# A modulation vector formed by row sums beside a feed-forward layer, and attention sinks as score columns

## The chip, the cores and the metric

The kernel runs on one core of one Trainium2 chip, in one launch. The metric is the device time in microseconds (us) of that launch. The kernel before was timed in three runs: 2712.57, 2717.24 and 2718.96 us, median 2717.24. One more execution was profiled. The engines are PE (TensorE; PEld is its weight load), DVE (VectorE), ACT (ScalarE), POOL (GpSimd) and SP (SyncE), which issues the weight loads. Sixteen DMA engines move data.

## The reference

Sequence 512, width 1024, all in float32. A first block has two layers. Layer 0 is feed-forward, an RWKV-7 time mix, feed-forward; layer 1 is feed-forward, sliding-window attention with sinks, feed-forward. A second block follows, whose normalization is modulated by a vector `mod` that depends on the input `c` alone. The two places that matter here:

```python
# in the attention: 16 heads, windows of 256 keys per 128 queries, one sink logit per head
sink = jnp.broadcast_to(sinks..., s.shape[:-1] + (1,))
p = jax.nn.softmax(jnp.concatenate([s, sink], axis=-1), axis=-1)[..., :-1]
o = jnp.einsum('bnkgqs,bnskd->bnqkgd', p, vb)

# at the start of the second block: c is (1, 1024), w_ada (1024, 3072)
mod = c @ w_ada[l] + b_ada[l]
shift, scale, gate = jnp.split(mod, 3, axis=-1)
h = rmsnorm(x, norm_gain[l]) * (1.0 + scale[:, None, :]) + shift[:, None, :]
...
x = x + gate[:, None, :] * (merged @ w_out[l])
```

## The kernel before, in words

Activations lie transposed: width over 128 partitions in 8 tiles of 512 positions. Weights come in units of 128x512 float32, 256 KB each. For each unit SP loads `w_raw` (a ring of 4), POOL splits it into a high part `w_hi` and the remainder `w_lo` (also rings of 4; lines L221, L222, L212), and PE multiplies: 4 output tiles by 3 products (high by high, high by low, low by high; L230, L231, L232), twelve matmuls per unit. `w_lo_ready` tells PE that a unit is split, `w_used` tells POOL that a place in the ring is free. DVE and ACT read the banks, apply norms and activations and split the results in the same way.

All engines run the layers in program order, each from its own written-out queue: feed-forward layers f0 to f3, the mix between f0 and f1, the attention `swa` between f2 and f3, the second block after f3. A feed-forward layer has 11 blocks of 8 units into `mid`, then 44 units of output projection in two halves. Its last three units are done bank by bank (`closing_products`, L250 to L252), so that a bank is complete early. The norm after a layer sums squares over partitions with matmuls against ones (L362), takes root and inverse, and spreads the inverse over partitions (L399). While this small chain runs, PE does a few matmuls whose results nobody reads (`unread`, L442). The next layer starts with `early_products` (L267, L268, L271), which take each tile as soon as DVE has updated it, and `norm_beside`, which puts the square sums of the next norm between products.

The attention runs 16 steps in a software pipeline. In iteration i, PE makes the scores of step i (L2017), transposes the probabilities of step i-3 (L2030) and multiplies the values of step i-4 (L2048). DVE adds the window mask and takes the row maximum (L2174, four per step), negates it (`neg`, L2179), adds the sink's exponential to the row sum (`den`, L2184), inverts it (`inv`, L2186) and copies half of the transposed probabilities (L2192). ACT takes the exponentials (L2119) and, for the sinks, two small ones of 128x2 per step (L2123), and copies the other half (L2112). POOL multiplies the probabilities by `inv` (L2216). All of POOL's divisions stand in its queue between two weight units.

The modulation vector is formed in the attention. `w_ada` is loaded by ACT's queue in 8 tiles of 128x3072 (rows of w_ada over partitions), two buffers. DVE multiplies each tile by a column of `c` and adds it to `ada_sum`, in four parts of 768 columns (L2154 for the first tile, L2151 for the others): 4 parts of tile 0 before the first step, 4 of tile 1 in iterations 0 and 1, one part in every second iteration from 4 to 18 (tiles 2 and 3), and the 16 parts of tiles 4 to 7 after the last step, beside the output projection of the attention. The sum over partitions is left to PE: 24 matmuls of `ada_sum` against one column of ones (L1996), each recorded as two. Ten stand among the norm chain at the end of the attention, each with an unread matmul (L1995), and 14 beside the first 7 units of f3. DVE then adds the bias (`mod`, L2222), and PE waits for that before `norm_beside` of f3 (`mod_ready`), because the bank is used again.

Of the kernel before, what the change touches and what calls it, by code (L numbers as in the profile page):

```python
# [64 lines left out]
def vector_table():  # L65
# [17 lines left out]
    c.add("c", KT)  # L83
# [37 lines left out]
def program(nc, xT, weights, vectors, masks_in, gather_in, spread_in, rows_in, window_in, ada_in, pos_in, rope_in, fold_in,  # L121
            tri_in, mask_a_in, mask_b_in, out):
    n_units = weights.shape[0]
    with ExitStack() as ctx:
# [457 lines left out]
        class Ffn:  # L582
            def __init__(self, number, layer, which, first_unit, x_tiles, updates, kv=None, after=None):
# [13 lines left out]
                self.after, self.inner = after, after is not None  # L597
                self.halved = {1: 1, 3: 3}.get(number, 0)

        def ffn_tensor(pe, s):  # L600
            odd = 1 - s.even

            def block(b, set_, n, i=None, k0=0):
                for k in range(k0, KT):
                    if b == 0 and s.kv is None:
                        early_products(pe, [o[:] for o in bank[set_]], k, s.x0, n + k, s.halved)
                        sum_square(pe, s.pre, k, bank[s.pre_at][0])
                        if s.after is not None and k < 7:
                            done = ada_products(pe, 10 + 2 * k, 12 + 2 * k)
                            if k == 6:  # L610
                                done.then_inc(ada_ready, 1)
# [85 lines left out]
        def ffn_scalar(act, s):  # L697
# [1255 lines left out]
        score = [mid_buffer(f"score{n}", [P, 2, 2, 2 * P]) for n in range(4)]  # L1953
        prob_t = [mid_buffer(f"prob_t{n}", [P, 2, T]) for n in range(2)]
        top, neg, total, sink_e, den, inv = (mid_buffer(n, [P, 4, 4]) for n in ("top", "neg", "total", "sink_e", "den", "inv"))
        ada_sum = mid_buffer("ada_sum", [P, 3 * D])
        ada_w = [mid_buffer(f"ada_w{n}", [P, 3 * D]) for n in range(2)]

        class Swa:
            def __init__(self, first_unit, x_tiles, updates):  # L1960
# [7 lines left out]
                self.after, self.inner, self.halved = None, False, 2  # L1968
# [3 lines left out]
        ada_ready = sem("ada_ready")  # L1972
        mod_ready = sem("mod_ready")
        qv = Steps("query_dve", [("q", k) for k in each])
        qa = Steps("query_act", [("bias", k) for k in each])
        av = Steps("ada_dve", [("ada", k, part_) for k in each for part_ in range(4)])
# [8 lines left out]
                               [(n, a) for a in step_at(i, 1) for n in ("den", "inv")] + [("turn", a) for a in step_at(i, 3)]])  # L1985
# [5 lines left out]

        def ada_products(pe, first, last, unread=None):
# [6 lines left out]
        def swa_tensor(pe, s):  # L1999
# [77 lines left out]
            for k in s.post.summed:  # L2077
                sum_square(pe, s.post, k, bank[s.post_at][0])
# [981 lines left out]
```

## Time and profile before

| | |
|---|---|
| runs, us | 2712.57, 2717.24, 2718.96 |
| the profiled execution, us | 2714.14 |
| its span, first to last instruction, us | 2712.0 |
| mean granted clock of TensorE | 0.985 |
| busy share of ACT, DVE, POOL | 23%, 40%, 72% |
| chain that ended last: PE, issue, DVE, POOL, ACT | 84%, 6%, 5%, 3%, 2% |
| loads of w_ada | 8 of 1536 KB, 7.0 us from issue to landing (median) |
| loads of weights | 778 of 256 KB, 2.6 us |

The span is what the rows below are read against; times in them are counted from its start. The busy share is an average over stages. A row of a timeline is start, length and operation; `[x <-Y]` behind it says that the engine sat idle for x us before it until Y had finished. Lengths of neighbouring instructions on one engine overlap a little, so distances between starts tell what one costs. In time, the attention with its query products lies at about 1676 to 1842 us and f3 behind it to about 2250 us. The granted clock is 1.00 where PE runs at the higher of its two levels.

### The profile page before, as it was taken

Reading aid. Unit: us, or ns where it says so; the run is one execution under the profiler, and the core shown is the slowest. Engines: PE = TensorE matmul, PEld = TensorE weight load, DVE = VectorE, ACT = ScalarE, POOL = GpSimd, SP = SyncE. Lnnn points to the kernel's source line nnn. Section 1 sums busy time; section 2 is a strip of 40 time slices with the busy share of each in tenths; the row PEclk is TensorE's granted clock in tenths of the full one; section 3 lists DMA queues with packets and bytes.
Section 4 is the critical chain, followed back from the end, with each engine's and each line's share of the span. In section 5 each row is a group of like instructions: output and inputs, shape, how many; then the busy total and the mean of one; then the engine's idle time right before and its main releaser. Section 6 shows DMA issues by size and latency. Waiting matters only on the chain.

```text
span 2712.0 us, 48113 instructions
## 1 busy us (share of the span) xinstructions
PE 2603.9 (96%) x17580; PEld 2116.9 (78%) x17580; DVE 1071.3 (40%) x1674; ACT 635.5 (23%) x1220; POOL 1956.0 (72%) x2573
## 2 busy tenths in 40 slices
PE   8999999988989999999999999889999999999998
PEld 6888887767877788888888888668888878777767
DVE  4222047884555622211522203876322233123354
ACT  2111025423443311101211102533111011354211
POOL 7888788873324688877788877676888858755675
PEclk9999999989999999999999999999999989999998
DMA  4333322210001233333333333342333323322212
GB/s 144 100 97 93 97 82 78 80 54 4 4 4 40 71 105 97 93 97 88 87 97 93 97 97 88 142 145 71 100 94 96 96 72 100 91 61 66 84 51 78
DMA packets 116790, 225.90 MB, mean 83 GB/s; under 512 B 13088, under 2 KB 13856, under 8 KB 115616
## 3 DMA queue, kind: packets, MB, share of 16 engines
q1 hardware_dynamic: 114624, 209.46, 26.6%
q10 hardware_dynamic: 2016, 14.22, 1.4%
q8 instruction: 121, 1.98, 0.3%
q14 instruction: 29, 0.24, 0.0%
HBM read 221.53 MB, written 2.10 MB: 82 GB/s over the span
## 4 chain that ended last, share of the span: by engine, by line
PE 84%; issue 6%; DVE 5%; POOL 3%; ACT 2%; DMA 0%; POOLq 0%; SPq 0%; DVEq 0%; ACTq 0%
PE bank L230 21%; PE bank L232 21%; PE bank L231 20%; PE bank L1480 1%; PE bank L362 1%; POOL w_hi L222 1%; PE bank L267 1%; PE bank L268 1%; PE bank L271 1%; POOL w_lo L212 1%; PE bank L1495 1%; PE bank L2462 1%; POOL w_hi L221 1%; PE bank L1430 1%; PE bank L1498 1%
## 5 line engine op out<-in xcount | busy, mean ns | idle before, releaser
L212 POOL TENSOR_TENSOR w_lo<-w_raw,w_hi 128x512 fp32r<-128x512 f32 x778 | 1051.5, 1352 | 63.6
L230 PE MATMUL bank<-x_hi,w_hi 128*128 128x512 f32 x1848 | 729.1, 395 | 6.3 <-POOL w_lo L212 4.3
L232 PE MATMUL bank<-x_hi,w_lo 128*128 128x512 f32 x1848 | 725.1, 392 | 0.0
L231 PE MATMUL bank<-x_lo,w_hi 128*128 128x512 f32 x1848 | 723.5, 391 | 0.0
L221 POOL TENSOR_TENSOR w_hi<-w_raw,ones 128x32 fp32r<-128x32 f32 x778 | 275.0, 354 | 452.6 <-PE bank L232 348.2
L222 POOL TENSOR_SCALAR w_hi<-w_raw 128x480 fp32r<-128x480 f32 x778 | 509.3, 655 | 0.0
L230 PEld LDWEIGHTS bank<-x_hi,w_hi 128*128 128x128 f32 x1848 | 347.5, 188 | 88.3 <-POOL w_lo L212 8.4
L232 PEld LDWEIGHTS bank<-x_hi,w_lo 128*128 128x128 f32 x1848 | 347.4, 188 | 76.1
L231 PEld LDWEIGHTS bank<-x_lo,w_hi 128*128 128x128 f32 x1848 | 347.5, 188 | 75.2 <-issue 0.2
L729 DVE TENSOR_TENSOR f<-bank,rstd 128x512 f32<-128x512 f32 x88 | 56.7, 686 | 624.0 <-PE bank L232 614.1
L232 PE MATMUL bank<-mid_hi,w_lo 128*128 128x512 f32 x656 | 257.2, 392 | 0.0
L231 PE MATMUL bank<-mid_lo,w_hi 128*128 128x512 f32 x656 | 256.8, 392 | 0.0
L230 PE MATMUL bank<-mid_hi,w_hi 128*128 128x512 f32 x656 | 256.2, 390 | 0.0
L705 ACT ACTIVATE f<-f 128x512 f32<-128x512 f32 x88 | 53.9, 632 | 717.5 <-DVE f L729 717.4
L231 PEld LDWEIGHTS bank<-mid_lo,w_hi 128*128 128x128 f32 x656 | 123.2, 188 | 27.4
L230 PEld LDWEIGHTS bank<-mid_hi,w_hi 128*128 128x128 f32 x656 | 123.2, 188 | 27.1
L232 PEld LDWEIGHTS bank<-mid_hi,w_lo 128*128 128x128 f32 x656 | 123.2, 188 | 26.3
L338 ACT ACTIVATE sq<-bank 128x512 f32<-128x512 f32 x35 | 20.4, 598 | 457.6 <-PE bank L232 224.0
L358 DVE TENSOR_TENSOR acc<-acc,sq 128x512 f32<-128x512 f32 x45 | 39.8, 885 | 209.1 <-ACT sq L338 208.8
L742 DVE TENSOR_TENSOR mid_lo<-f,mid_hi 128x512 f32 (+1 forms) x88 | 101.7, 1182 | 11.0 <-ACT mid_hi L710 10.9
L510 DVE TENSOR_SCALAR f<-bank,vec 128x512 f32<-128x512 f32 x20 | 14.9, 743 | 223.8 <-ACT sq L338 223.8
L1718 POOL TENSOR_TENSOR e_mat<-mab,masks 128x512 f32<-128x512 f32 x40 | 50.7, 1273 | 64.5 <-PE bank L1480 39.0
(479 smaller groups left out, 3669.9 us busy)
## 6 DMA issues: line engine op xcount, KB each, us to landing
w_raw<-weights SPq DMA_DIRECT2D x778, 256.0 KB, 2.6
ada_w<-ada_in ACTq DMA_DIRECT2D x8, 1536.0 KB, 7.0
h<-xT SPq DMA_DIRECT2D x4, 512.0 KB, 6.7
out<-f SPq DMA_DIRECT2D x8, 256.0 KB, 2.2
mask_b<-mask_b_in ACTq DMA_DIRECT2D x1, 640.0 KB, 3.9
spread<-spread_in SPq DMA_DIRECT2D x1, 512.0 KB, 7.8
window<-window_in ACTq DMA_DIRECT2D x1, 512.0 KB, 5.0
masks<-masks_in SPq DMA_DIRECT2D x1, 320.0 KB, 7.7
```

The source lines that it names most:

```text
L212: pool.tensor_tensor(w_lo[:, (n - 1) % RW, :], w_raw[:, (n - 1) % RS, :], w_hi[:, (n - 1) % RW, :].bitcast(F32), ALU.subtract).then_inc(w_ ...
L221: pool.tensor_tensor(w_hi[:, n % RW, 0:HEAD], w_raw[:, n % RS, 0:HEAD], ones[:, 0:HEAD], ALU.mult)
L222: pool.tensor_scalar(w_hi[:, n % RW, HEAD:], w_raw[:, n % RS, HEAD:], 1.0, 0.0, ALU.mult, ALU.add).then_inc(w_hi_ready, 1)
L230: pe.matmul(outs[m], w_hi[:, s, c], hi, start=first, stop=False)
L231: pe.matmul(outs[m], w_hi[:, s, c], lo, start=False, stop=False)
L232: done = pe.matmul(outs[m], w_lo[:, s, c], hi, start=False, stop=last)
L267: pe.matmul(o[:, t], w_hi[:, s, c], x_hi[:, k, t], start=k == 0 and t.start == 0, stop=False)
L358: dve.tensor_tensor(acc[:], acc[:], square_at(nm, j), ALU.add).then_inc(sq_used, 1)
L705: act.activation(g_buf[:, p, :], g_buf[:, p, :], ACT.Silu).then_inc(silu_ready, 1)
L729: dve.tensor_tensor(g_buf[:, p, :], bank[set_][p][:], rstd[:], ALU.mult).then_inc(bank_read, 1)
L742: dve.tensor_tensor(lo, u_buf[:, p, :], hi.bitcast(F32), ALU.subtract).then_inc(mid_lo_ready, 1)
L1718: pool.tensor_tensor(e_mat[:, u], mab[:, u], masks[:, l:l + 1, :].to_broadcast([P, 8, CH]), ALU.mult).then_inc(*cg.tell("e", m, l, u))
```

## The change

**The modulation.** `w_ada` is now laid out transposed: 24 tiles of 128x1024, where each partition holds one output of `mod` and its row of 1024 weights. `c` comes as a tile `cond`, repeated on all partitions. One `tensor_tensor_reduce` of 128x1024 on DVE multiplies a tile by `cond` and sums along the row, which gives one column of `mod`. This is done in f3: ACT loads `cond` and two tiles before its first block; behind each of the ten looped blocks DVE has two products and ACT two loads, each behind a wait for the product that frees the buffer; the last four products, the bias and the gain of the second block's norm stand behind the loop on DVE. In the loop the sums go through the small tile `root2` to `mod`. The matmuls against ones, their bank and the two waits for it go; the end of the attention now uses the same `output_tensor` as the other layers.

**The sinks.** Each row of the score tile gets one more column. DVE copies the sinks of the step's heads there before the mask (128x4, L2146 of the kernel after); the exponential of ACT runs over 257 columns instead of 256 and its row sum then includes the sink. The two exponentials of 128x2 and the addition `den` go.

```diff
         def norm_beside(pe, s, outs, n, last):
-            if s.after is not None:
-                pe.wait_ge(s.after, 1)
...
         def ffn_tensor(pe, s):
                         early_products(pe, [o[:] for o in bank[set_]], k, s.x0, n + k, s.halved)
                         sum_square(pe, s.pre, k, bank[s.pre_at][0])
-                        if s.after is not None and k < 7:
-                            done = ada_products(pe, 10 + 2 * k, 12 + 2 * k)
...
         def ffn_scalar(act, s):
+            if s.inner:
+                act.dma_start(cond[:], cond_in).then_inc(cond_loaded, 16)
+                for n in two:
+                    ada_load(act, n)
             block(0)
             with act.Fori(0, (FB - 1) // 2) as i:
                 for j in range(2):
                     block(1 + j, i)
+                    for n in two if s.inner else ():
+                        act.wait_ge(ada_done, count(2 * j + n + 1, i, 4))
+                        ada_load(act, 2 * j + n + 2, i)
+            if s.inner:
+                for n in range(LOOPED + 2, ADA):
+                    act.wait_ge(ada_done, n - 1)
+                    ada_load(act, n)
...
         def ffn_vector(dve, s):
             block(0, s.even)
+            if s.inner:
+                dve.wait_ge(cond_loaded, 16)
+                dve.memset(root2[:], 0.0).then_inc(ada_kept, 1)
             with dve.Fori(0, (FB - 1) // 2) as i:
-                block(1, 1 - s.even, i)
-                block(2, s.even, i)
+                for j, set_ in enumerate((1 - s.even, s.even)):
+                    block(1 + j, set_, i)
+                    for n in two if s.inner else ():
+                        ada_product(dve, 2 * j + n, i)
+            if s.inner:
+                for n in range(LOOPED, ADA):
+                    ada_product(dve, n)
+                ada_vector(dve)
...
-        score = [mid_buffer(f"score{n}", [P, 2, 2, 2 * P]) for n in range(4)]
+        score = [mid_buffer(f"score{n}", [P, 2, 2, 2 * P + 16]) for n in range(4)]
...
         def swa_tensor(pe, s):
-            pe.wait_ge(f_ready, s.h0 // 2 + 4)
-            pe.wait_ge(*av("ada", KT - 1, 3))
-            norm_sums(pe, s.post, bank[s.post_at][0])
-            for k in s.post.summed:
-                sum_square(pe, s.post, k, bank[s.post_at][0])
-            ada_products(pe, 0, 2, bank[SETA][3])
-            norm_wide(pe, s.post, bank[s.post_at][1])
-            ada_products(pe, 2, 10, bank[SETA][0])
+            output_tensor(pe, s)
...
         def swa_scalar(act, s):
                     for j in two:
                         for t in two:
-                            act.activation(score[a % 4][:, j, t, :], score[a % 4][:, j, t, :], ACT.Exp, ...)
-                    for j in two:
-                        c = KV + 2 * (a // 2) + j
-                        done = act.activation(sink_e[:, a % 4, 2 * j:2 * j + 2], neg[:, a % 4, 2 * j:2 * j + 2], ACT.Exp, bias=rows[:, c:c + 1])
+                            with_sink = score[a % 4][:, j, t, 0:2 * P + 1]
+                            done = act.activation(with_sink, with_sink, ACT.Exp, ...)
...
         def swa_vector(dve, s):
-            for part_ in range(4):
-                ada(0, part_)
...
+                    sinks = rows[:, KV + 2 * r:KV + 2 * r + 2].rearrange("p (j t s) -> p j t s", t=1, s=1).to_broadcast([P, 2, 2, 1])
+                    dve.tensor_copy(score[a % 4][:, :, :, 2 * P:2 * P + 1], sinks)
...
-                    dve.tensor_tensor(den[:, a % 4, :], total[:, a % 4, :], sink_e[:, a % 4, :], ALU.add).then_inc(*ad.tell("den", a))
-                    dve.wait_ge(*ad("den", a))
-                    dve.reciprocal(inv[:, a % 4, :], den[:, a % 4, :]).then_inc(*ad.tell("inv", a))
+                    dve.reciprocal(inv[:, a % 4, :], total[:, a % 4, :]).then_inc(*ad.tell("inv", a))
...
-                if i < 2:
-                    ada(1, 2 * i)
-                    ada(1, 2 * i + 1)
-                elif i % 2 == 0 and 4 <= i <= 18:
-                    ada(2 + (i - 4) // 8, (i - 4) // 2 % 4)
             low(KT - 1)
-            for k in range(4, KT):
-                for part_ in range(4):
-                    ada(k, part_)
             output_vector(dve, s)
...
+        def ada_product(dve, n, i=None):
+            dve.wait_ge(ada_loaded[n % 2], count(16 * (n // 2 + 1), i, 32))
+            total_ = mod[:, n:n + 1] if i is None else root2[:, n:n + 1]
+            if i is not None and n == 0:
+                dve.wait_ge(ada_kept, count(1, i, 1))
+            dve.tensor_tensor_reduce(out=ada_w[n % 2][:], in0=ada_w[n % 2][:], in1=cond[:], scale=1.0, scalar=0.0, op0=ALU.mult, op1=ALU.add,
+                                     accum_out=total_).then_inc(ada_done, 1)
+            if i is not None and n == 3:
+                dve.wait_ge(ada_done, count(4, i, 4))
+                dve.tensor_tensor(mod[:, bass.ds(i * 4, 4)], root2[:], ones[:, 0:4], ALU.mult).then_inc(ada_kept, 1)
```

DVE in the attention, from the end of one step to the first mask operation of the next, before (`score_136` and so on are the four score buffers, `ISA` is the masking operation or the read of its maximum):

```order
L2179 TENSOR_SCALAR neg<-top 128x4
L2184 TENSOR_TENSOR den<-total,sink_e 128x4
L2186 RECIPROCAL inv<-den 128x4
L2192 COPY prob_t_141<-bank 128x512
L2151 SCALAR_TENSOR_TENSOR ada_sum<-ada_w_149,vec,ada_sum 128x768
L2174 ISA score_137,top<-bank,window,rows 128x256
```

and the same place in the changed kernel:

```order
L2154 TENSOR_SCALAR neg<-top 128x4
L2159 RECIPROCAL inv<-total 128x4
L2165 COPY prob_t_141<-bank 128x512
L2146 COPY score_139<-rows 128x4
L2149 ISA score_139,top<-bank,window,rows 128x256
```

The addition and the accumulation are gone, and a copy of the sinks stands in front of each step's first mask operation, behind the inverse that lets POOL start.

PE at the end of the attention, from the square sums to the first products of f3, before:

```order
L362 MATMUL bank<-ones,acc 128x64 x4
L362 MATMUL bank<-ones,sq_last 128x64 x4
L1995 MATMUL bank<-ones,ident 128x128
L1996 MATMUL bank<-ones,ada_sum 128x1
L1995 MATMUL bank<-ones,ident 128x128
L1996 MATMUL bank<-ones,ada_sum 128x1
L399 MATMUL bank<-ident,rinv 128x128 x4
L1995 MATMUL bank<-ones,ident 128x128
L1996 MATMUL bank<-ones,ada_sum 128x1
```

and in the changed kernel:

```order
L438 MATMUL bank<-ones,ident 128x128
L361 MATMUL bank<-ones,acc 128x64 x4
L361 MATMUL bank<-ones,sq_last 128x64 x4
L438 MATMUL bank<-ones,ident 128x128 x2
L398 MATMUL bank<-ident,rinv 128x128 x4
L438 MATMUL bank<-ones,ident 128x128 x6
L266 MATMUL bank<-x_hi,w_hi 128x256
```

Before, eight pairs of an unread matmul and a modulation product follow the spread inverse (the last row shown begins them); now six unread matmuls do, and f3's products come next.

## Rows read from the trace of the kernel before

**Rows 1.** The page's first part: busy us (share of the span), instructions.

```profile
PE 2603.9 (96%) x17580; PEld 2116.9 (78%) x17580; DVE 1071.3 (40%) x1674; ACT 635.5 (23%) x1220; POOL 1956.0 (72%) x2573
```

**Rows 2.** Two windows: us, busy us (instructions) by engine, clock, DMA share, GB/s.

```profile
1750.00:1780.00 30.00, 24.38 (x210) 16.88 (x208) 28.18 (x109) 27.23 (x103) 18.58 (x36) 1.00 0.15 54
1900.00:2000.00 100.00, 100.00 (x438) 82.05 (x438) 25.71 (x34) 10.45 (x17) 84.09 (x113) 1.00 0.34 98
```

**Rows 3.** The waits of PE, 1680 to 1900 us: line, releaser, total, times, longest.

```profile
PE bank L2030 <- DVE q_t L2144: 5.4, 1, 5.4
...
PE bank L250 <- POOL w_lo L212: 3.8, 2, 2.0
...
PE bank L230 <- DVE mod L2222: 1.8, 1, 1.8
```

**Rows 4.** Timeline of DVE, two steps of the attention: start, us, operation, [idle before].

```profile
1754.07 1.03 DVE L2151 SCALAR_TENSOR_TENSOR ada_sum<-ada_w,vec,ada_sum 128x768 f32<-128x768 f32 x1
...
1756.75 0.17 DVE L2179 TENSOR_SCALAR neg<-top 128x4 f32<-128x4 f32 x1
1756.83 0.16 DVE L2184 TENSOR_TENSOR den<-total,sink_e 128x4 f32<-128x4 f32 x1
1757.03 0.18 DVE L2186 RECIPROCAL inv<-den 128x4 f32<-128x4 f32 x1
...
1760.88 1.02 DVE L2151 SCALAR_TENSOR_TENSOR ada_sum<-ada_w,vec,ada_sum 128x768 f32<-128x768 f32 x1
```

**Rows 5.** Timeline of PE and DVE, the head of the attention.

```profile
1727.35 2.00 PE L2017 MATMUL bank<-k_sh,q_t 64*128 64x256 f32 x16
...
1729.93 0.47 DVE L2174 CUSTOM_DVE_ANT_0 score<-bank,window,rows 128x256 f32<-128x256 f32 x1
...
1734.78 1.54 PE L2030 MATMUL bank<-ident,score 128*128 128x128 f32 x6 [5.43 <-DVE q_t L2144]
```

**Rows 6.** Timeline of POOL and DVE where both read SBUF in the attention.

```profile
1730.44 1.62 POOL L2216 TENSOR_SCALAR score<-score,inv 128x128 f32<-128x128 f32 x4
...
1731.65 0.43 DVE L2179 TENSOR_SCALAR neg<-top 128x4 f32<-128x4 f32 x1
...
1753.66 2.61 POOL L2216 TENSOR_SCALAR score<-score,inv 128x256 f32<-128x256 f32 x4 [1.54 <-DVE inv L2186]
```

**Rows 7.** The tile ada_sum, DVE's row: ns min/median/max; then POOL's timeline.

```profile
L2151 DVE SCALAR_TENSOR_TENSOR ada_sum<-ada_w,vec,ada_sum x28: 1006/1056/2066, 1722.6 to 1817.0; 128x768 f32<-128x768 f32 x28
...
1796.74 0.25 POOL L221 TENSOR_TENSOR w_hi<-w_raw,ones 128x32 fp32r<-128x32 f32 x1 [1.85 <-PE bank L232]
...
1818.24 0.97 POOL L221 TENSOR_TENSOR w_hi<-w_raw,ones 128x32 fp32r<-128x32 f32 x1
```

**Rows 8.** Timeline of PE, the output projection of the attention.

```profile
1793.57 0.50 PE L230 MATMUL bank<-x_hi,w_hi 128*128 128x512 f32 x1
...
1823.92 0.51 PE L250 MATMUL bank<-x_hi,w_hi 128*128 128x512 f32 x1 [1.77 <-POOL w_lo L212]
...
1826.91 0.79 PE L250 MATMUL bank<-x_hi,w_hi 128*128 128x512 f32 x1 [2.02 <-POOL w_lo L212]
```

**Rows 9.** Timeline of PE, square sums that end one layer and open the next.

```profile
1671.64 1.00 PE L362 MATMUL bank<-ones,acc 128*128 128x64 f32 x8
...
1704.44 1.10 PE L362 MATMUL bank<-ones,acc 128*128 128x64 f32 x8 [1.36 <-DVE acc L358]
...
1835.45 1.00 PE L362 MATMUL bank<-ones,acc 128*128 128x64 f32 x8
...
1873.68 1.00 PE L362 MATMUL bank<-ones,acc 128*128 128x64 f32 x8
```

**Rows 10.** The tile ada_sum, PE's row; then POOL in the last feed-forward layer.

```profile
L1996 PE MATMUL bank<-ones,ada_sum x48: 166/250/250, 1837.6 to 1864.5; 128*128 128x1 f32 x48
...
1904.61 0.25 POOL L221 TENSOR_TENSOR w_hi<-w_raw,ones 128x32 fp32r<-128x32 f32 x1
...
1906.77 0.25 POOL L221 TENSOR_TENSOR w_hi<-w_raw,ones 128x32 fp32r<-128x32 f32 x1
```

More of the change, by code:

```diff
@@ L82, in vector_table @@
     c.add("final", KT)
-    c.add("c", KT)
     return c
@@ L582, in program, with __init__ @@
         class Ffn:
-            def __init__(self, number, layer, which, first_unit, x_tiles, updates, kv=None, after=None):
+            def __init__(self, number, layer, which, first_unit, x_tiles, updates, kv=None, inner=False):
                 self.kv, self.rs = kv, new_rstd()
@@ L596, in __init__ @@
                 self.pre, self.post = Norm(KT, () if kv is None else ODD, kept=True), Norm(KT, (7,), late=True)
-                self.after, self.inner = after, after is not None
+                self.inner = inner
                 self.halved = {1: 1, 3: 3}.get(number, 0)
@@ L1967, in __init__ @@
                 self.gain_in, self.gain_out, self.bias, self.half, self.kv = "norm12", "norm13", "b_o", 1.0, None
[L1968 removed]
+                self.inner, self.halved = False, 2
         window_loaded = sem("window_loaded")
         ada_loaded = [sem(f"ada_loaded{n}") for n in range(2)]
[L1972 to L1973 removed]
+        cond_loaded = sem("cond_loaded")
+        ada_done = sem("ada_done")
+        ada_kept = sem("ada_kept")
         qv = Steps("query_dve", [("q", k) for k in each])
         qa = Steps("query_act", [("bias", k) for k in each])
[L1976 removed]
         STEPS = 2 * KT
@@ L1990, in swa_blocks @@
             return [(t, kt) for t, kt in (((0, 0), (1, 0), (1, 1)) if x == 0 else ((0, 0), (0, 1), (1, 0), (1, 1)))]
-        def ada_products(pe, first, last, unread=None):
-            for m in range(first, last):
-                if unread is not None:
-                    pe.matmul(unread[:, 0:P], ident[:], ones[:], start=True, stop=True)
-                done = pe.matmul(bank[SETA][2][:, m:m + 1], ada_sum[:, m * P:(m + 1) * P], ones[:, 0:1], start=True, stop=True)
-            return done
         def swa_tensor(pe, s):
@@ L2295, in program @@
         pa = Steps("proj_act", ["sin"] + [(n, m) for n, tiles in PROJ + BESIDE + GATES for m in range(tiles)])
-        pv = Steps("proj_dve", ["gain"] + [("norm", k) for k in each] +
+        pv = Steps("proj_dve", ["mod", "gain"] + [("norm", k) for k in each] +
                    ["float", "angle", "near", "steps", "less1", "less2", "less3", "phase", "clip", "one"])
@@ L2369, in second_vector @@
         def second_vector(dve, s):
-            dve.scalar_tensor_tensor(out=gain_s[:], in0=mod[:, KT:2 * KT], scalar=1.0, in1=vec[:, VEC.at["gain2"]:VEC.at["gain2"] + KT],
-                                     op0=ALU.add, op1=ALU.mult).then_inc(*pv.tell("gain"))
             dve.wait_ge(*ip("wide"))
@@ L2835, in program @@
         swa = Swa(f2.end, 8 * KT, 4)
-        f3 = Ffn(3, 1, 1, swa.end, 10 * KT, 5, after=mod_ready)
+        f3 = Ffn(3, 1, 1, swa.end, 10 * KT, 5, inner=True)
         second = Second(f3.end, 11 * KT, 6)
```

58 lines of the change are left out of this document (23 added, 35 removed).

## The prediction

> **What bounds the kernel now.** I read the page's busy shares first, then windows by stage, then the waits of PE, then timelines of the stages that the change touches. PE is busy for 96% of the span [rows 1], so nearly all work elsewhere is free, and only two kinds of time can be won: PE's own instructions and the few stretches in which PE stands still or in which an engine sets its pace. In the last feed-forward layer PE has no gap: 438 matmuls in 100 us, so a unit of twelve takes 2.74 us [rows 2]. In the attention it is different. From 1750 to 1780 us PE is busy for 24.38 of 30 us, DVE for 28.18 and ACT for 27.23 [rows 2]: DVE sets the pace there. The waits of PE around the attention show three that involve the modulation: 5.4 us at the attention's head for a query that DVE writes late, 3.8 us for POOL's low weights in the output projection, 1.8 us for the tile mod at the start of the last feed-forward layer [rows 3].
>
> **Part 1: the attention's loop (saves 3.5 us).** In the loop DVE works without a gap, and the distance between two modulation steps, which is two attention steps, is 1760.88 - 1754.07 = 6.81 us [rows 4]. The change takes out of such a pair one accumulation (1.0 us) and two additions that form the denominator (from 1756.83 to 1757.03, 0.20 us each [rows 4]), and adds two copies of the sinks, 128x4, which I price like the negation of the same size, 1756.75 to 1756.83, 0.08 us from start to start [rows 4]. DVE's own work falls to 6.81 - 1.00 - 0.40 + 0.16 = 5.57 us. The copies have a hidden price. POOL's division of a step takes 1.62 or 2.61 us in four instructions [rows 6], 4.23 us per pair, so POOL is working in about two thirds of the loop, and the copy stands just where it works: behind inv, which starts it. The negation that fell into such a division, at 1731.65, took 0.43 us, against 0.17 us outside one [rows 4, 6]. So a small operation waits for the POOL instruction under way, 0.41 or 0.65 us long. I take 0.3 us per copy, 0.6 us per pair; nothing and 0.65 us per copy are the ends. That gives 6.2 us of DVE per pair. The other engines leave room: PE's share gives 24.38 / 30 x 6.81 = 5.5 us, and ACT's gives 6.2 us, from which the two pairs of sink exponentials go. Because the chain crosses from DVE to ACT and back, I take 0.5 us saved per pair, not 0.6. Eight accumulations stand in the loop with seven distances between them, so 3.5 us. Ends: 0 (ACT or the chain keeps the old pace) to 7 x 1.0 = 7 us (copies never blocked).
>
> The Trainium skill (SBUF — State Buffer, Who interferes with whom) says that a copy or a scalar operation in a two-port mode takes the port pair that VectorE shares with GpSimd for the whole instruction, and whoever is second is blocked until the first is done. The trace agrees for the negation, 0.43 against 0.17 us. A copy from SBUF to SBUF is of that kind, so by this rule the copies are the part of the change that speaks against it; without the rule the part would be worth the 7 us of its upper end.
>
> **Part 2: the head of the attention (saves 1.5 us).** Four accumulations leave DVE in the first two steps. PE waits 5.43 us until 1734.78 for the last queries, which DVE scales after the third step's scores [rows 5]. The third mask began at 1729.93, while its scores, the first half of sixteen matmuls from 1727.35 that took 2.00 us, were there at about 1728.4 [rows 5]. Everything behind it on DVE can move up by that 1.5 us only; the rest of the wait stays. Ends: 0.5 and 2.5 us (two denominators go too, and POOL no longer loses time to the first accumulations).
>
> **Part 3: the output projection (saves 6.0 us).** From 1793.57 to the square sums at 1835.45 lie 41.88 us [rows 8, 9]; 13 weight units are in it, which at 2.74 us are 35.6 us. The loss is 6.3 us. It has one cause, and the change removes it: sixteen accumulations and more run back to back on DVE from there, and under them POOL needed 1818.24 - 1796.74 = 21.5 us for six units, 3.58 us each [rows 7], where a unit without them takes 1906.77 - 1904.61 = 2.16 us [rows 10]. At 3.58 us POOL is slower than PE's 2.74, uses up its lead, and PE waits 1.77 and 2.02 us [rows 8]. Behind the second wait a matmul's record is 0.79 us instead of 0.51: the rest of the loss is matmuls at the lower clock. Without the accumulations POOL is the faster one, and next in line is nothing but PE itself. 6.0 us; ends 3.8 (waits alone) and 6.3.
>
> **Part 4: the passage into the last feed-forward layer (saves 5.0 us).** Before, 24 products of 128x1 (48 recorded matmuls, 0.25 us each [rows 10]) stand on PE: ten between fillers and fourteen beside the first units, and then PE waits 1.8 us for mod [rows 3]. The passage from the feed-forward layer into the attention has the same code without them. From square sums to square sums it takes 1704.44 - 1671.64 = 32.80 us; the one at hand takes 1873.68 - 1835.45 = 38.23 us [rows 9]. The difference, 5.4 us, is what can go. What is late next is DVE's sum of squares, as the 1.36 us wait at 1704.44 shows [rows 9]; since DVE works at its own speed there I hold back 0.4 us. Ends: 1.8 (the wait for mod alone) and 5.4.
>
> **Part 5: the last feed-forward layer (costs nothing).** DVE gets 24 multiply-and-sum operations of 128x1024, two per block of eight units. None is in the trace; by length the accumulation of 768 columns gives 1.06 x 4/3 = 1.4 us, at its slowest 2.07 x 4/3 = 2.8 us [rows 7]. DVE is busy for a quarter of this layer [rows 2], and PE needs a bank read only one block, 21.9 us, later, so DVE's time is hidden. POOL's is the question. In the projection it lost 6 x (3.58 - 2.16) = 8.5 us under 21.5 us of accumulations, 0.40 us per us. Two operations of 1.4 us then cost POOL 1.1 us per block, at worst 2.2 us; it is busy for 84.09 of 100 us [rows 2], which leaves 3.5 us per block. Hidden. If the cover went, every us beyond 3.5 would cost 11 blocks x 1 us. The loads are 1 MB per block, 48 GB/s on top of 98 [rows 2]. They are issued by ACT, which now waits for DVE's product behind each block; behind that wait stand the next block's silu operations, whose inputs come from DVE behind the same product, so nobody waits longer. The last four products, the addition of the bias and the gain stand on DVE before output_vector, 44 units (120 us) before PE's square sums: hidden. Ends: a gain is excluded (work is only added); loss up to the case of the third rival.
>
> The same page and section say that an operation with two SBUF inputs, as the multiply-and-sum is, blocks a GpSimd instruction that reads SBUF, for its full length. By that rule POOL would lose up to 2.8 us per block instead of 1.1, still under the spare 3.5, so the sum stays; the third rival is that rule with slower operations. The rows show 0.40 us lost per us, not 1, because both engines have gaps and DVE waits as well.
>
> **Sum.** 3.5 + 1.5 + 6.0 + 5.0 = 16.0 us, all on PE's path, because behind it PE has no slack until the end. The profiled execution took 2714.14 us (span 2712.0): 2698.1 us. The median of the runs, 2717.24 us, is 3.1 us above that execution, which would give 2701.2. I predict 2700 us.
>
> **Rivals.** First, the copies of the sinks are not blocked by POOL: DVE's pair is then 5.57 us and the chain through ACT and PE about 5.8, so the loop saves 7 x 1.0 = 7 us: 2696. For it: a negation in the loop is short, 0.17 us [rows 4]; against it: that one stands before inv, when POOL has finished, and the copy stands after. Second, DVE's relief doesn't reach PE, in the loop or in the passage: ACT, busy for 27.23 of 30 us, keeps the loop's pace, or the sum of squares keeps most of the passage. Then only 0 to 1 us of part 1 or 1.8 us of part 4 remain: 2703 with one of them, 2706 with both. ACT's high share speaks for it, the removed exponentials against. Third, on the other side: in the last feed-forward layer the new operations run at the slow end, 2.8 us each, and shut POOL out for their full length. 5.6 us per block against 3.5 us spare is 2.1 us x 11 = 23 us lost, PE waits for low weights throughout: 2700 + 23 = 2723, slower than before. It decides from 1.75 us of POOL's time per operation on. The slowest accumulation in rows 7 speaks for such lengths, the 0.40 measured under the densest stretch against.
>
> **Chances.** Forecast 0.55, first rival 0.17, second 0.22, third 0.06. A measurement of this kernel tells about 0.2%, 5.4 us, from no change, so faster means under 2711.8. The first two rivals are faster too. The forecast's ends sum to savings of 6 and 21 us, which are hardly reached together. Range 2692 to 2710. Faster 0.91, same 0.05, slower 0.04 (part of the third rival falls short of it).
>
> **What would show it.** The distance of two prob_t copies of one kind in the attention near 6.3 us, and copies of the sinks with records of 0.3 us or more; first transposes at about 1733.3; no wait for w_lo in the output projection, with square sums 35.9 us after the unit that began at 1793.57; 33 us from there to the next square sums; in the last feed-forward layer no wait of PE for w_lo beyond what was there, POOL busier by some 5 of 100 us. I would be wrong if PE waits for w_lo in that layer, if the loop's pace stays at 6.8 us, or if a new wait stands in the passage.

## The result, and the profile after

The changed kernel takes 2680.2 us (median of 4 runs, 2677.0 to 2687.6) against 2714.9 us before (4 runs, 2711.9 to 2719.0): ratio 0.987, 95% interval 0.985 to 0.989. Faster was right; the time of 2700 us was 20 us too high, and 2680 us lies outside the range of 2692 to 2710. The profiled execution took 2679.1 us, its span 2677.3 us, 34.7 us less than the one before.

First the page's busy shares after the change. PE is still busy for 96% of the span, but for 26.0 us less than before [rows 1], of which the removed products of the modulation (48 recorded matmuls of 0.25 us, [rows 10]) explain 12 us at most. That was the first sign that something else had changed.

```profile
PE 2577.9 (96%) x17530; PEld 2108.5 (79%) x17530; DVE 1071.9 (40%) x1696; ACT 629.2 (24%) x1188; POOL 1959.0 (73%) x2573
```

Next the two windows that answer to [rows 2]: 30 us inside the attention's loop and 100 us of the last feed-forward layer; the columns are us, busy us (instructions) of PE, PEld, DVE, ACT and POOL, clock, DMA share, GB/s.

```profile
1730.00:1760.00 30.00, 29.42 (x256) 20.64 (x254) 28.66 (x128) 26.66 (x94) 16.86 (x39) 1.00 0.01 2
1900.00:2000.00 100.00, 100.00 (x443) 82.81 (x442) 40.58 (x56) 11.21 (x18) 91.07 (x113) 1.00 0.50 146
```

The first line goes the way that was forecast, and further: the loop gets 256 matmuls through in the time of 210, where a pair of steps in 6.3 instead of 6.81 us would give 227. PE is busy for 29.42 of the 30 us there, against 24.38 before, so the loop now runs nearly as fast as PE's own work allows. The second line was not forecast: PE was without a gap before and is without a gap now, and yet it does 443 matmuls instead of 438, beside more work of DVE and POOL, not less. The first feed-forward layer, which stands 1300 us ahead of anything that the change moves, shows the same (next fence: 200 us of it, before and then after).

```profile
100.00:300.00 200.00, 200.00 (x876) 1.00 0.33 96
...
100.00:300.00 200.00, 200.00 (x884) 1.00 0.34 97
```

The waits of PE from 1660 to 1850 us answer to [rows 3]: those for w_lo in the projection and for mod are gone (0.3 us are left), the one for q_t fell from 5.4 to 3.7 us.

```profile
PE bank L2036 <- DVE q_t L2129: 3.7, 1, 3.7
PE bank L361 <- DVE acc L357: 2.8, 2, 1.4
...
PE bank L229 <- POOL w_lo L211: 0.3, 1, 0.3
```

Last, the timeline of PE at the stages' borders, the counterpart of [rows 5, 8, 9].

```profile
1659.96 1.00 PE L361 MATMUL bank<-ones,acc 128*128 128x64 f32 x8
...
1692.64 1.10 PE L361 MATMUL bank<-ones,acc 128*128 128x64 f32 x8 [1.44 <-DVE acc L357]
...
1722.32 0.90 PE L2036 MATMUL bank<-ident,score 128*128 128x128 f32 x3 [3.71 <-DVE q_t L2129]
...
1777.15 0.50 PE L229 MATMUL bank<-x_hi,w_hi 128*128 128x512 f32 x1
...
1812.88 1.00 PE L361 MATMUL bank<-ones,acc 128*128 128x64 f32 x8
...
1845.49 1.10 PE L361 MATMUL bank<-ones,acc 128*128 128x64 f32 x8 [1.37 <-DVE acc L357]
...
2181.91 1.00 PE L361 MATMUL bank<-ones,acc 128*128 128x64 f32 x8
```

When the attention begins, the changed kernel is already 11.7 us ahead (1659.96 against 1671.64). From border to border the 34.7 us come to: 14.4 us in the four feed-forward layers (3.2, 4.7, 3.4 and 3.1), 10.8 us in the attention (131.01 to 120.24), 5.6 us in the passage (38.23 to 32.61), 3.5 us behind the last feed-forward layer, 0.4 us elsewhere. The attention and the passage are where the forecast had its 16 us; the rest was not in it.

### The profile page after: what moved, and what is told of

The parts are those of the page before. It is cut to its first block, busy times and chain, and to the rows that moved or that the text cites. A ratio compares the mean times of both kernels' runs of the same rounds, so it can differ in the third digit from the quotient of the medians.

```text
span 2677.3 us, 48059 instructions
## 1 busy us (share of the span) xinstructions
PE 2577.9 (96%) x17530; PEld 2108.5 (79%) x17530; DVE 1071.9 (40%) x1696; ACT 629.2 (24%) x1188; POOL 1959.0 (73%) x2573
## 4 chain that ended last, share of the span: by engine, by line
PE 84%; issue 5%; DVE 5%; POOL 3%; ACT 2%; DMA 0%; POOLq 0%; SPq 0%; DVEq 0%; ACTq 0%
PE bank L229 21%; PE bank L230 21%; PE bank L231 21%; PE bank L1492 1%; PE bank L361 1%; POOL w_lo L211 1%; POOL w_hi L221 1%; PE bank L266 1%; PE bank L1507 1%; PE bank L267 1%; PE bank L270 1%; PE bank L2448 1%; PE bank L1442 1%; PE bank L1510 1%; PE bank L2439 1%
## 5 line engine op out<-in xcount | busy, mean ns | idle before, releaser
L337 ACT ACTIVATE sq<-bank 128x512 f32<-128x512 f32 x35 | 20.4, 598 | 441.5 <-PE bank L251 218.8
L745 DVE TENSOR_TENSOR mid_lo<-f,mid_hi 128x512 f32 (+1 forms) x88 | 101.2, 1176 | 11.1 <-ACT mid_hi L702 10.9
```

The lines of the kernel that those rows point to most:

```text
L745: dve.tensor_tensor(lo, u_buf[:, p, :], hi.bitcast(F32), ALU.subtract).then_inc(mid_lo_ready, 1)
```

## The experiments

**Theory A.** A line of the diff that the part shown above leaves out takes the entry `c` out of the vector table (`c.add("c", KT)`); 279 columns become 271, and the tile `vec` shrinks from 1152 to 1088 bytes. Every tile behind it in SBUF moves by 64 bytes: x_hi from byte 70080 to 70016, mid_hi from 119232 to 119168. The weights, ahead of it, stay at 41088 and 49280. A matmul of 512 columns then costs less because of where its moving operand starts. **Theory B:** the pace is the chip's or the instruction stream's, not the placement's. The first four runs separate them. Each group of runs was made beside runs of the kernel before, whose median was 2713.8 to 2720.4 us from group to group; so a few us between versions of different groups say little, and the count of matmuls in the same 200 us (from 100 to 300 us, inside the first feed-forward layer) tells more.

e1, the kernel before with eps behind the tables:

```diff
-        eps = sb("eps", [P, 1])
...
         out_bias = sb("out_bias", [P, KT])
+        eps = sb("eps", [P, 1])
```

> The kernel before with nothing changed but the place of one small table (eps) in SBUF, so that x_hi, x_lo and the middle values, the moving operands of the 512-column matmuls, start at a multiple of 128 bytes (byte 70016 instead of 70080) as they do in the changed kernel, while the weights keep their bytes. Theory A (18 us of the saving come from the moving operands' addresses, which the shorter vector table shifted): about 18 us less than before, 2697 us, with 443 instead of 438 matmuls of PE in 100 us of a feed-forward layer. Theory B (the faster matmul comes from the chip's state or from the instruction stream of the changed program): the time of before, 2715 us.

Measured: 2703.0 us (2699.5 to 2705.9) against 2713.8, ratio 0.996 (0.9945 to 0.9973), and 884 matmuls in the 200 us. The four feed-forward layers are 14.4 us shorter; its mix layer took 498.6 us against 492.9, which took part of it back in the profiled execution. Over all profiles of this study that layer lies between 489.7 and 502.8 us without a pattern in the placements. A holds; its 18 us was too much for this run.

e2, the changed kernel with the old addresses. This is the clean measure of what the change does by itself.

```diff
         vec = sb("vec", [P, VEC.n])
+        place[0] += 64
```

> The changed kernel with 64 bytes left empty behind the vector table, so that every tile behind it has the address of before. Theory A (addresses): about 18 us more than the changed kernel, 2698 us, which is what the change's own parts give (16 us less than before). Theory B (state or instruction stream): 2680 us as the changed kernel.

Measured: 2699.3 us (2694.1 to 2701.8), ratio 0.995 (0.9935 to 0.9968), 19 us above the changed kernel. The feed-forward layers are back at 876 matmuls, as before. B is out. The borders of its stages, for the forecast's own terms:

```profile
1704.69 0.77 PE L362 MATMUL bank<-ones,acc 128*128 128x64 f32 x5 [1.35 <-DVE acc L358]
...
1732.93 1.54 PE L2037 MATMUL bank<-ident,score 128*128 128x128 f32 x6 [3.72 <-DVE q_t L2130]
...
1774.39 0.50 PE L230 MATMUL bank<-x_hi,w_hi 128*128 128x512 f32 x1
...
1823.68 0.89 PE L362 MATMUL bank<-ones,acc 128*128 128x64 f32 x7
...
1856.41 1.10 PE L362 MATMUL bank<-ones,acc 128*128 128x64 f32 x8 [1.29 <-DVE acc L358]
...
2196.04 1.00 PE L362 MATMUL bank<-ones,acc 128*128 128x64 f32 x8
```

e3 moves the middle values alone, e4 the weights alone (the line stands before `w_hi`; eps goes behind the tables, so that x stays):

```diff
         f = sb("f", [P, KT, T])
+        place[0] += 64
```
```diff
+        place[0] += 64
         w_hi = sb("w_hi", [P, RW, UC], F32R)
```

> The changed kernel with x_hi and x_lo where they are, and only the middle values (mid_hi, mid_lo, the moving operand of every second-half unit of a feed-forward layer) moved by 64 bytes. Theory A, by the share of matmuls that read the middle values (about 1970 of some 8000, 2.6 ns each): 5 us more than the changed kernel, 2685 us, lost in the second half of each feed-forward layer alone. Theory B: 2680 us. A third theory, that it is another tile behind the vector table: 2680 us here, 2698 us in the run beside it.

> The changed kernel with x and the middle values where they are, and w_hi and w_lo, the stationary operands, moved by 64 bytes. If only the moving operand's start counts, 2680 us as the changed kernel. If the weight side counts as much as the moving one, its loads are hidden beside the matmuls before them, so at most some us: up to 2700 us when a weight load's reads collide in the same way.

Measured: e3 2682.6 us (2679.9 to 2684.9), 882 matmuls, its first feed-forward layer 337.5 us against 336.3 (after) and 339.5 (before): the loss stays with the matmuls that read the middle values. e4 2731.1 us (2730.6 to 2735.6), 859 matmuls, slower than the kernel before. So the weights' place counts, and more than x's, which no theory had.

**Theory R**, that only the distance between the two operands counts, against A (each for itself). e5 puts 64 bytes before w_hi and leaves all behind it shifted too; e6 puts the tile mod (128 bytes) there; e7 orders the small tables so that ident, ones, masks, spread and gather start at multiples of 128; e8 moves x and the middle values by 32.

```diff
+        place[0] += 64                     # e5, before w_hi
...
+        mod = sb("mod", [P, 3 * KT])       # e6, before w_hi
...
+        eps = sb("eps", [P, 1])            # e7, before ident
+        place[0] += 128                    # e7, before masks, instead of 64
+        gain_s = sb("gain_s", [P, KT])     # e7, before spread; it also moves gn_eps of the mix layer
...
+        place[0] += 32                     # e8, before sq; again before masks
```

> The changed kernel with 64 bytes left empty before w_hi, so that the weights and everything behind them, x and the middle values too, start 64 bytes off a multiple of 128. Moving x alone cost 19 us and moving the weights alone cost 51 us. Theory A (each operand pays for its own start): more than 2731 us, about 2750 us if the prices add up. Theory R (only the distance between the two operands counts): 2680 us, as the changed kernel, where both start at a multiple of 128.

> The changed kernel with 128 bytes more before w_hi, so that weights, x and middle values start at multiples of 256 (before: 128 past one). If a multiple of 128 is all that counts: 2680 us. If a still wider boundary counts: less, and more than 443 matmuls in 100 us of a feed-forward layer; one of 512 columns every 0.2257 us against 0.2133 us for 512 columns at 2.4 GHz leaves room for up to 100 us.

> The changed kernel with its small tables put in another order, so that nearly every tile of 512 bytes and more starts at a multiple of 128 (identity, ones, masks, spread, gather are added to x, the middle values and the weights). If starts matter for small matmuls, transposes and vector operations too: some us less than the changed kernel, 2672 to 2678 us, won between 405 and 898 us (the mix layer). If only the 512-column matmuls' operands matter: 2680 us.

> The changed kernel with x and the middle values 32 bytes past a multiple of 64, the weights as they are. If the price goes by whether the start is a multiple of 128: as with 64 bytes, 2699 us. If it goes by 64-byte pieces that a read touches: more than that, up to 2720 us.

Measured: e5 2677.5 us (2676.3 to 2683.8), ratio 0.9855 (0.9836 to 0.9875), and 884 matmuls, with both operands 64 past a multiple of 128. A falls in its first form: no start is good or bad by itself. R holds. e6 2684.1, e7 2683.6 us: neither a wider boundary nor aligned small tables are worth anything. e8 2734.2 us.

e9 and e10 split the change by its parts: e9 is the changed kernel with the sinks handled as before, e10 the kernel before with the sinks as score columns.

```diff
-                    dve.tensor_copy(score[a % 4][:, :, :, 2 * P:2 * P + 1], sinks)     # e9; e10 adds it
...
+                    dve.tensor_tensor(den[:, a % 4, :], total[:, a % 4, :], sink_e[:, a % 4, :], ALU.add).then_inc(*ad.tell("den", a))
```

> The changed kernel with the sinks handled as before (no copies of them into the scores, two exponentials of 128x2 per step on ACT, an addition before the reciprocal), the modulation and all addresses of x, middle values and weights as in the changed kernel. By the prediction's first part the sinks' new form costs DVE 0.2 us more per pair of steps than it takes away (0.6 against 0.4), so without it the loop is 1.4 us shorter: 2679 us. By the rival (the saved exponentials of ACT and the short copies are what made the pace 5.95 instead of 6.3 us per pair): 0.35 us per pair more, 2683 us.

> The kernel before with the sinks as score columns, the modulation left in the attention, and the vector table left at its length, so that all starts are those of before. By the prediction: 1.4 us more in the loop, 2716 us, and no change in a feed-forward layer (438 matmuls in 100 us). If the faster matmul came with the sinks' part of the change: 2697 us. If copies are cheap: 2 us less, 2713 us.

Measured: e9 ratio 0.988 (0.9864 to 0.9903), which can't be told from the changed kernel's 0.987; by borders its attention takes 120.75 us against 120.24, and the profiles of the six other versions with the changed kernel's instructions there and distance 0 lie between 120.26 and 120.35. e10 ratio 1.000 (0.9989 to 1.0013), 875 matmuls in 200 us. The sinks are worth 0.5 us once the modulation is gone. While the modulation is there they bring nothing that can be measured: e10's attention took 132.98 us against 131.01, but the passage behind it 36.84 against 38.23, and e1, with the sinks as before, had 132.46 us in the attention. Its copies of the sinks had a median of 0.30 us against 0.21 in the changed kernel. So within the noise all of the change's own gain is the modulation.

e11 and e12 reach two more distances from x's side (small tables moved from ahead of x to behind out_bias: eps and root, or eps alone).

```diff
-        eps = sb("eps", [P, 1])                # e11 and e12: from ahead of sq
-        root = sb("root", [P, TT])             # e11 alone
...
         out_bias = sb("out_bias", [P, KT])
+        eps = sb("eps", [P, 1])
+        root = sb("root", [P, TT])
```

> The changed kernel with x and the middle values 128 bytes lower, the weights as they are: the distance from w_hi to x_hi is 128 past a multiple of 256. Theory P128 (the distance counts modulo 128): 2680 us and 443 matmuls in 100 us. Theory P256 (it counts modulo 256; +64 cost 19 us, -64 cost 51 us, so they are not alike): another number than 443, between 430 and 442, 2685 to 2735 us.

> The changed kernel with x and the middle values 64 bytes lower and the weights as they are: the same distance (-64) as in the run that moved the weights up by 64, reached from the other side. If the distance decides, as the run with both shifted says: 2731 us and 430 matmuls in 100 us of a feed-forward layer. If the place of the weights themselves cost the 51 us there: 2699 us and 438, as with x moved up.

Measured (one run each): e11 2721.3 us, 862 matmuls in 200 us; e12 2732.9 us, 859, as in e4, which has the same distance from the other side. The period is not 128.

e13 moves x by 1280 bytes (vec, eps, root and rinv go behind out_bias), e14 by 32 and e15 by 160, all downwards. e16 puts one more product ahead of each product of the modulation.

```diff
-        vec = sb("vec", [P, VEC.n])            # e13; it also moves eps, root and rinv
-        eps = sb("eps", [P, 1])                # e14; e15 moves eps, root and rinv
+        place[0] += 32                         # e14 and e15, before sq
...
+            dve.tensor_tensor_reduce(out=spare[:, 0:896], in0=ada_w[n % 2][:, 0:896], in1=cond[:, 0:896], scale=1.0, scalar=0.0, op0=ALU.mult,
+                                     op1=ALU.add, accum_out=spare[:, 896:897]).then_inc(spare_done, 1)
```

> The changed kernel with x and the middle values 1280 bytes lower (some small tables stand behind them now), the weights as they are: the distance from w_hi to x_hi is a multiple of 512, not 256 past one as in the changed kernel. Period 256: 2680 us and 443 matmuls in 100 us. Period 512 with a still better place: fewer us than 2676, over 443 matmuls. Period 512 with 256 as the good place: 430 to 440 matmuls, 2695 to 2735 us.

> The changed kernel with x and the middle values 32 bytes lower: distance -32 from that of the changed kernel. So far +32 cost 54 us, +64 19 us, -64 51 us, -128 41 us. If only multiples of 64 and more are good places: 430 matmuls in 100 us, 2733 us. If the price grows with the distance below 0: 436 to 440, about 2705 us.

> The changed kernel with x and the middle values 160 bytes lower: distance -160, which is +96 with a period of 256. If places that are no multiple of 64 are all bad: 430 matmuls in 100 us and 2733 us. If the price is a smooth curve between +64 (438) and +128 (432): 435 matmuls, about 2712 us.

> The changed kernel with each of the 24 products of the last feed-forward layer preceded by another one of 896 columns, whose result nobody reads. By the prediction's last part GpSimd has 3.5 us to spare per block of 21.9 us and loses about 1.1 us to two products, so that four still hide: 2680 us, the layer 336.4 us, GpSimd near 97 of 100 us. By the third rival (each product shuts GpSimd out for its full length, 1.3 us here): 4 x 1.3 = 5.1 us per block, 1.6 us over the spare time, 11 blocks: 17 us more, 2697 us, with waits of PE for w_lo.

Measured: e13 2685.2 us (2683.9 to 2686.3), 884 matmuls: the period is 256. e14 2733.0, e15 2737.6 us (one run each). e16 2693.7 us (2691.0 to 2698.3), the last feed-forward layer 347.35 us against 336.42: the cover of part 5 does run out. 100 us of that layer and the waits of PE in it:

```profile
2000.00:2100.00 100.00, 95.69 (x412) 78.03 (x412) 66.48 (x85) 11.27 (x17) 97.17 (x101) 0.98 0.48 142
...
PE bank L229 <- POOL w_lo L211: 7.8, 8, 1.8
```

POOL is full at 97 of 100 us, PE waits for low weights 8 times, and some of what follows runs at a lower granted clock (0.98). The forecast had given 2680 us here, the third rival 2697.

e17 moves w_lo alone by 64 bytes (eps behind the tables, so that x stays), e18 the mix layer's own buffers.

```diff
+        place[0] += 64                                                              # e17
         w_lo = sb("w_lo", [P, RW, UC], F32R)
...
+        where["r_arr"] = where["mid_hi"] + 64                                       # e18
```

> The changed kernel with w_lo alone moved up by 64 bytes, w_hi, x and the middle values as they are. All three matmuls of a product were 0.0070 us slower when both weights were moved. Theory L (a load of weights collides with the stream of the matmul before it): only the load of w_lo, which happens under the stream of x_lo in the matmul x_lo, w_hi, is at the bad distance, and a third of the 51 us is lost: 2697 us, 438 or 439 matmuls in 100 us, with one of the three records longer. Theory O (the distance between the two operands of one matmul counts, with the weights read again during it): also a third, but the longer one is the matmul x_hi, w_lo. Theory S (any operand off its place slows all): 2731 us.

> The changed kernel with the mix layer's own buffers (r, k, v, u and what follows them) moved up by 64 bytes, which took them where the third run had them, and x, the middle values and the weights of all feed-forward layers at the good distance. The third run's mix layer took 489.7 us against 492.7 us. If that was placement: 3 us less than the changed kernel, 2677 us. If it was chance: 2680 us and more, the layer anywhere between 490 and 502 us as in the other runs.

Measured: e18 2683.8 us (2681.3 to 2686.1), its mix layer 497.3 us: e3's 489.7 was chance. e17 2722.2 us (one run), 867 matmuls. None of its three theories had that: one load in three is moved, and it loses 17 matmuls, where moving all weights lost 25. PE's groups in 200 us (line, operands, count, busy us, mean ns of one):

```profile
L232 PE MATMUL bank<-x_hi,w_lo 128*128 128x512 f32 x229 | 91.0, 397 | 0.0
L231 PE MATMUL bank<-x_lo,w_hi 128*128 128x512 f32 x228 | 89.4, 392 | 0.0
L230 PE MATMUL bank<-x_hi,w_hi 128*128 128x512 f32 x228 | 88.7, 389 | 0.0
```

The matmul that uses w_lo and the one under which w_lo is loaded are longer, the third has the 389 ns of the changed kernel. All loads keep 188 ns. The price sits where w_lo is involved; whether the load or the stream is held up is left open.

All placements together, x's start less w_hi's, modulo 256 (all four moving tiles and both weights have the same one, except in e17, and in e3, which is not in the table: x at 0, the middle values at 64, 882 matmuls, 337.5 us):

| distance | matmuls in 200 us | first feed-forward layer, us | runs |
|---|---|---|---|
| 0 | 884 | 336.3 | changed kernel, e1, e5, e6, e7, e9, e13, e16, e18 |
| 32 | 859 | 345.9 | e8 |
| 64 | 875 or 876 | 339.5 | kernel before, e2, e10 |
| 96 | 858 | 345.9 | e15 |
| 128 | 862 | 344.5 | e11 |
| 192 | 859 | 345.9 | e4, e12 |
| 224 | 859 | 345.9 | e14 |
| 0, w_lo 192 | 867 | 342.7 | e17 |

160 was not tried. The period rests on e11, which rules out 128, and on e13, which moves x by five times 256. No version measured beats the changed kernel: the ratios of e5, e7, e13 and e18 (0.9855 to 0.9876) have intervals that overlap its 0.987.

## Why the prediction was wrong

**The step that failed** is the sum: it took the five parts from the time before and left every other us as it was, "because behind it PE has no slack until the end". The diff's shorter vector table is an edit that the prediction gave no term. It has one: in the profiled spans 14.9 us (2692.2 of e2 less 2677.3), by the medians 19 us. Without it the changed kernel is e2, 2699.3 us, where the prediction said 2700; that they agree to a microsecond is in part luck, since the terms below were off by up to 0.6 us each and the kernel before ran at 2713.8 us beside e2, where the prediction started from 2717. The busy share of 96% was read as work that nothing could shorten. But a unit of twelve matmuls at 2.74 us was itself a slow one: 12 x 200 / 876 = 2.740 us, and 12 x 200 / 884 = 2.715 us at the good distance.

The forecast's own terms, best read on e2 (its borders above against [rows 5, 8, 9]):

- **Part 1, the loop**, forecast 3.5: 45.55 to 41.46 us, 4.1 saved. The loop ends where the first unit of the output projection starts; that line of the kernel before is:

```profile
1780.33 0.50 PE L230 MATMUL bank<-x_hi,w_hi 128*128 128x512 f32 x1
```

  The size is near, but by luck. Seven pairs were to save 0.5 us each. The copies of `prob_t`, one per step, show what happened (next fence: two copies of one kind in the kernel before, then two in e2). A pair fell from 6.81 us, in places 7.15, to 6.13 and 5.78 us, not to 6.3: over nine steps in the middle, 31.21 us (from 1746.68 to 1777.89) became 26.73 us (from 1745.20 to 1771.93), 1.0 us saved per pair. The first three steps gave 0.5 us back (9.94 us became 10.44), with PE at its lower clock from 1731.5 to 1738.3 us in e2, twice as long as before.

```profile
1753.48 0.68 DVE L2192 COPY prob_t<-bank 128x512 f32<-128x512 f32 x1
...
1760.29 0.68 DVE L2192 COPY prob_t<-bank 128x512 f32<-128x512 f32 x1
...
1757.09 0.69 DVE L2166 COPY prob_t<-bank 128x512 f32<-128x512 f32 x1
...
1763.22 0.69 DVE L2166 COPY prob_t<-bank 128x512 f32<-128x512 f32 x1
```

  So the pace came near the first rival's 5.8 us, and PE is nearly without a gap at it. The copies were priced at 0.3 us; over all 16 their median is 0.208 us, the longest 0.580. The timeline of DVE and POOL shows both lengths, each time while POOL is at its divisions:

```profile
1749.71 1.62 POOL L2181 TENSOR_SCALAR score<-score,inv 128x128 f32<-128x128 f32 x4 [1.10 <-DVE inv L2159]
1750.61 0.30 DVE L2146 COPY score<-rows 128x4 f32<-128x4 f32 x1
...
1752.89 1.85 POOL L2181 TENSOR_SCALAR score<-score,inv 128x256 f32<-128x256 f32 x4 [1.55 <-DVE inv L2159]
1753.33 0.16 DVE L2146 COPY score<-rows 128x4 f32<-128x4 f32 x1
```

  So a copy is longer at times, not always; the first rival had the better part of the truth. The second rival is wrong: DVE's relief reached PE.
- **Part 2, the head**, forecast 1.5: 30.34 to 28.24 us, 2.1 saved. In the changed kernel it is only 0.7: there PE's clock fell for a while behind its wait at 1692.64, shown by records of 0.63 us instead of 0.39 and starts 0.43 us apart instead of 0.23 (the lower of the two levels, 1.2 GHz; the granted clock reads 0.50 from 1694.0 to 1697.3 us). Eight matmuls at 0.2 us each are the 1.6 us that e2 doesn't lose. The change's instructions don't cause this, but its placement goes with it: all nine profiles with x and the middle values at distance 0 have the stretch, e1 with the instructions of before among them, and none of the eleven others. Why the clock falls there was not followed up. A term of that size hides under it.

```profile
1694.67 0.63 PE L229 MATMUL bank<-x_hi,w_hi 128*128 128x512 f32 x1
1695.10 0.63 PE L230 MATMUL bank<-x_lo,w_hi 128*128 128x512 f32 x1
...
1698.18 0.39 PE L231 MATMUL bank<-x_hi,w_lo 128*128 128x512 f32 x1
1698.41 0.39 PE L229 MATMUL bank<-x_hi,w_hi 128*128 128x512 f32 x1
```

- **Part 3, the output projection**, forecast 6.0: from the loop's end to the square sums 55.12 to 49.29 us, 5.8 saved, with 0.3 us of waits for w_lo left. Right, in place and size.
- **Part 4, the passage**, forecast 5.0: 38.23 to 32.73 us, 5.5 saved. DVE's sum of squares is late next by 1.3 us, as it was said; the 0.4 us held back were not needed.
- **Part 5, the last feed-forward layer**, forecast 0: 339.48 to 339.63 us. Right in the result, half right in the size. A product takes 1.26 to 2.35 us, median 1.57 (forecast 1.4 to 2.8). For POOL the next fence has the whole layer, before and after, with the same 365 instructions of POOL in it; so 24 products cost POOL 295.05 - 274.68 = 20.4 us, 0.85 us each, not 0.55. That is 1.7 us per block against 3.5 to spare. With four per block (e16) nothing is to spare, and the layer gets 10.9 us longer: the third rival was right that the cover can run out, and it lay one doubling away. Its price was too high: by e16's expectation its rule gave 17 us, and a further product cost POOL (317.19 - 295.05) / 24 = 0.92 us, not its full length.

```profile
1873.68:2213.16 339.48, 338.59 (x1485) 277.43 (x1484) 88.92 (x112) 37.10 (x60) 274.68 (x365) 1.00 0.32 94
...
1845.49:2181.91 336.42, 335.54 (x1485) 277.35 (x1485) 130.59 (x168) 37.09 (x60) 295.05 (x365) 1.00 0.45 134
```

The terms sum to 4.1 + 2.1 + 5.8 + 5.5 - 0.15 = 17.4 us, forecast 16.0. e2's span is 19.8 us shorter than before. Behind the last feed-forward layer it gains 2.7 us, elsewhere it loses 0.3; neither was followed up. By the medians e2 gains 14.4 us (8.7 to 17.6 by its interval).

## What to carry to other kernels

When an engine is busy without a gap, its pace is still a number to explain: count its instructions per us in a stretch that the change doesn't touch, before and after, ahead of any story on the stretch that it does. A diff that resizes one small table moves every tile behind it; print the addresses of both kernels, and keep them fixed (here by 64 empty bytes) when a change is to be judged by itself. On a kernel bound by 512-column matmuls, try the distance between stationary and moving tiles first: it is one line, and between the best and the worst place it was some 55 us here, about three times what the change's own parts were worth (17.4 us by their terms).

## What the runs showed of the hardware that was not expected

A matmul's pace depends on the distance in SBUF between its weights and its moving operand, modulo 256 bytes: 0.2262 us (200 / 884) at distance 0, 0.2283 at 64, 0.2320 at 128, 0.2328 to 0.2331 at 32, 96, 192 and 224, for 128x512 fp32r operands in a stream in which each load of 188 ns lies under the matmul before it. The starts by themselves don't matter (e5). Which access is held up is not known. The Trainium skill (SBUF — State Buffer, Who interferes with whom) gives PE two independent read ports, one for the moving operand and one for loading weights, and says that only the port pair shared by VectorE and GpSimd causes contention. By that rule all placements would have run in 2680 us; e4 and e8 took 2731 and 2734, so here the measurement decides.

The same section lets a VectorE operation with two SBUF inputs block GpSimd for its full length. Of a median product of 1.57 us POOL lost 0.85 us, so about half; each further product of e16 cost it 0.92 us. The rule is an upper bound here; a reason for the half that isn't lost was not tested.
